# Moving loads, copies and convolution taps between the steps of the first attention in a two-block transformer kernel

## The reference, cut to what matters

```python
h = rmsnorm(x, g_mix)
z = h @ w_in
zb, zc, zx, zq, zk, zv = split(z)              # six pieces of 512 columns
y_c = zb * causal_dwconv3(zc * zx, conv_w, conv_b)
q, k = rmsnorm per head(zq), rmsnorm per head(zk); v = zv      # 8 heads of 64
y_a = dilated_attention(q, k, v)               # 3 branches, merged by their weights
y = concat([rmsnorm(y_c, g_out_conv), rmsnorm(y_a, g_out_attn)])
x = x + y @ w_out
# causal_dwconv3(u, w, b) = u[t-2]*w[0] + u[t-1]*w[1] + u[t]*w[2] + b
```

## Time and profile before

| | us |
|---|---|
| median of 3 runs | 2587.83 |
| the profiled execution | 2583.64 |
| its span | 2582.0 |
| busy in the span: PE, PEld | 2516.0, 2088.5 |
| busy: DVE, ACT, POOL | 1361.7, 1055.3, 1265.2 |

### The profile page before, as it was taken

One profiled execution on the slowest core, in us unless ns is written; L12 is line 12 of the kernel. 1 busy time (PEld: TensorE's weight loads), 2 busy tenths in 40 slices (PEclk: granted clock), 3 DMA queues, 4 the chain that ended last, 5 costly groups with the idle time before them and its releaser, 6 DMA issues.

```text
span 2582.0 us, 34606 instructions
## 1 busy us (share of the span) xinstructions
PE 2516.0 (97%) x12210; PEld 2088.5 (81%) x12210; DVE 1361.7 (53%) x2479; ACT 1055.3 (41%) x1951; POOL 1265.2 (49%) x940
## 2 busy tenths in 40 slices
PE   8989999999999999999999999889999999999999
PEld 6877878888888888888877777689888888888887
DVE  5327766188766762225267888777247333333222
ACT  6336653253333332224256666586234333322120
POOL 2122323457766665534525554454356666656441
PEclk9999999999999999999999999999999999999999
DMA  4253432312222244210323212320412222226311
GB/s 157 75 170 117 116 82 83 146 58 106 90 82 88 77 160 175 82 65 27 107 74 94 66 62 70 108 69 21 155 74 74 82 85 79 82 105 222 114 45 70
DMA packets 107402, 246.28 MB, mean 95 GB/s; under 512 B 18880, under 2 KB 40672, under 8 KB 106976
## 3 DMA queue, kind: packets, MB, share of 16 engines
q1 hardware_dynamic: 107232, 244.08, 27.9%
HBM read 184.27 MB, written 55.05 MB: 93 GB/s over the span
## 4 chain that ended last, share of the span: by engine, by line
PE 87%; DVE 4%; ACT 2%; issue 2%; DMA 2%; POOL 2%; SPq 1%; ACTq 0%; DVEq 0%; POOLq 0%
PE PS L965 10%; PE PS L964 10%; PE PS L963 10%; PE PS L701 8%; PE PS L703 8%; PE PS L702 8%; PE PS L981 6%; PE PS L982 6%; PE PS L983 6%; PE PS L1233 2%; PE PS L1213 1%; PE PS L806 1%; PE PS L933 1%; PE PS L935 1%; PE PS L934 1%
## 5 line engine op out<-in xcount | busy, mean ns | idle before, releaser
L701 PE MATMUL PS<-Hh,Wl 128*128 128x512 f32 x1072 | 434.3, 405 | 12.0 <-DVE Hl L1364 9.4
L703 PE MATMUL PS<-Hh,Wh 128*128 128x512 f32 x1072 | 420.7, 392 | 0.0
L702 PE MATMUL PS<-Hl,Wh 128*128 128x512 f32 x1072 | 420.3, 392 | 0.0
L3220 POOL TENSOR_TENSOR Wl<-Wr,Wh 128x512 fp32r<-128x512 f32 (+1 forms) x158 | 209.4, 1346 | 336.0 <-ACT Wh L2320 335.7
L3323 POOL TENSOR_TENSOR RG<-RW,RG 128x512 fp32r<-128x512 f32 x176 | 246.9, 1408 | 130.2 <-ACT RG L2631 130.0
L1807 DVE TENSOR_TENSOR XA<-PS,XA 128x512 f32<-128x512 f32 x192 | 132.4, 691 | 332.5 <-PE PS L983 332.5
L981 PE MATMUL PS<-Hh,RG 128*128 128x512 f32 x704 | 274.1, 389 | 1.6 <-POOL Hl L3419 1.2
L983 PE MATMUL PS<-Hh,RG 128*128 128x512 f32 x704 | 273.9, 389 | 0.0
L982 PE MATMUL PS<-Hl,RG 128*128 128x512 f32 x704 | 273.9, 389 | 0.0
L3323 POOL TENSOR_TENSOR RG<-SW,RG 128x512 fp32r<-128x512 f32 x120 | 165.3, 1377 | 171.5 <-ACT RG L2631 147.0
L965 PE MATMUL PS<-Hh,RG 128*128 128x512 f32 x640 | 249.0, 389 | 0.0
(11 more groups left out here) (365 smaller groups left out, 5145.6 us busy)
## 6 DMA issues: line engine op xcount, KB each, us to landing
RW<-in_wg SPq DMA_DIRECT2D x44, 512.0 KB, 3.7
RW<-in_wu SPq DMA_DIRECT2D x44, 512.0 KB, 4.6
R<-in_wd SPq DMA_DIRECT2D x88, 256.0 KB, 3.0
hgscr<-GB SPq DMA_DIRECT2D x44, 512.0 KB, 2.6
G<-hgscr SPq DMA_DIRECT2D x40, 512.0 KB, 6.8
Wr<-in_wi SPq DMA_DIRECT2D x27, 512.0 KB, 3.4
Wr<-in_wo SPq DMA_DIRECT2D x16, 512.0 KB, 3.3
spill<-X SPq DMA_DIRECT2D x16, 512.0 KB, 2.6
```

Source lines behind the costliest of these rows:

```text
L701: pe.matmul(ps(b), k.Wl[:, s, wc], xh[:, kx, sl], start=kk == 0, stop=False)
L702: pe.matmul(ps(b), k.Wh[:, s, wc], xl[:, kx, sl], start=False, stop=False)
L703: i = pe.matmul(ps(b), k.Wh[:, s, wc], xh[:, kx, sl], start=False, stop=kk == nk - 1)
L3220: i = pool.tensor_tensor(k.Wl[:, s, c], k.Wr[:, s, c], k.Wh[:, s, c].bitcast(F32), ALU.subtract)
```

## The change

On SyncE the keys of head 1 are loaded before the value tiles are stored. On ScalarE the exponential goes ahead of `next_head`; the next head's keys are copied in two halves, at i = 3 and i = 4; `use` stands behind the first step of a unit; the convolution's first tap is an Identity activation with the tap as scale and the bias as bias; the squares stand behind later steps. On VectorE the first tap is gone and taps 1 and 0 and the two products with b are spread over steps of the b unit and the next c unit. GpSimd's additions and SyncE's store of `YC` follow. For j = 3 the order stays nearly as it was.

```diff
 vector: conv_x
-        if half == 0:
-            return
-        ...waits...
-        dve.tensor_scalar(y, k.ZC[:, 2:T + 2], col("conv_w", 8 + j), col("conv_b", j), ALU.mult, ALU.add).then_inc(
-            *up("conv", "cv", 0, j))
 vector: the loop over units
-                taps = {2: lambda j=j: conv_tap(j, 1), 6: lambda j=j: conv_tap(j, 0)} if (c, half) == ("b", 0) else {}
-                walk(8, 2, taps, tick)
+                later = {}
+                if (c, half) == ("c", 0) and j:
+                    later = {2: lambda j=j, b=b: conv_b(j - 1, 1, b)}
+                if (c, half) == ("b", 0):
+                    if j < 3:
+                        later = {6: lambda j=j: conv_tap(j, 1)}
+                    else:
+                        later = {2: lambda j=j: conv_tap(j, 1), 6: lambda j=j: conv_tap(j, 0)}
+                if (c, half) == ("b", 1) and j < 3:
+                    later = {2: lambda j=j: conv_tap(j, 0), 4: lambda j=j, b=b: conv_b(j, 0, b)}
+                walk(8, 2, later, tick)
 scalar: the head's copies
+    def key_part(h, z):
+        if z == 0:
+            act.wait_ge(*at("k1_in", h, 1))
+        return act.activation(k.KSa[h % 2][:, half_of(z)], k.KSr[:, half_of(z)], ACT.Copy)
 next_head:
+        if i == 3 and h < 7:
+            key_part(h + 1, 0)
         if i == 4 and h < 7:
-            key_high(h + 1)
+            key_part(h + 1, 1).then_inc(*up("q_hi", "k1_hi", h + 1))
 scalar: attention1
-            if s < n:
-                next_head(s)
             if 1 <= s <= n:
                 ...exponential of s-1...
+            if s < n:
+                next_head(s)
 scalar: new
+    def conv_first(j):
+        ...the waits that VectorE had, and zx...
+        act.activation(k.YC[:, j % 2, :], k.ZC[:, 2:T + 2], ACT.Identity, bias=k.col("conv_b", j),
+                       scale=k.col("conv_w", 8 + j)).then_inc(*up("tap0", "cv", 0, j))
+    def conv_square(j, half):
+        staged = [("v2_in", 0, 7), ("v_kept", 7)] if (j, half) == (1, 0) else []
+        square("conv", j, half, k.YC[:, j % 2, half_of(half)], staged + [("yb", j, half)])
 scalar: the loop over units
-            use()
             for half in range(2):
-                walk(8, 2, {}, tick)
+                later = {}
+                if half == 0:
+                    later[2] = use
+                if (c, half) == ("b", 0):
+                    if j < 3:
+                        later[4] = lambda j=j: conv_first(j)
+                    else:
+                        conv_first(j)
+                if (c, half) == ("c", 0) and j:
+                    later[6] = lambda j=j: conv_square(j - 1, 1)
+                walk(8, 2, later, tick)
                 b = bank.next()
+                if (c, half) == ("b", 1) and j < 3:
+                    conv_square(j, 0)
 gpsimd: the loop over units
-                if c == "b" and 0 < j < 3:
-                    add("conv", j, half)
-                    pool.wait_ge(*at("acc", "conv", half, j))
+                if (c, half) == ("b", 1) and 0 < j < 3:
+                    add("conv", j, 0)
+                    pool.wait_ge(*at("acc", "conv", 0, j))
+                if (c, half) == ("c", 0) and 0 < j - 1 < 3:
+                    add("conv", j - 1, 1)
+                    pool.wait_ge(*at("acc", "conv", 1, j - 1))
 sync: tables1
-            if i == 0 and h < 7:
+            if i == 0 and 0 < h < 7:
                 key_load(h + 1)
 sync: before the loop that stores the value tiles
+    key_load(1)
 sync: the store of YC moves from the end of j to the first half of the next j's c unit
+                if (c, half) == ("c", 0) and j:
+                    sp.wait_ge(*at("yb", j - 1, 1))
+                    sp.dma_start(d["yscr"][j - 1], k.YC[:, (j - 1) % 2, :]).then_inc(
+                        *up(("d_ys", j - 1), "yc_stored", j - 1))
```

More of the change, by code:

```diff
@@ L1569, in vector @@
                 if c == "b":
-                    conv_b(j, half, b)
                     if j == 3:
+                        conv_b(j, half, b)
                         add("conv", 3, half, k.sq_no["conv", half, 3])
@@ L2472, in key_high @@
     def key_high(h):
-        act.wait_ge(*at("k1_in", h, 1))
-        act.activation(k.KSa[h % 2][:, :], k.KSr[:, :], ACT.Copy).then_inc(*up("q_hi", "k1_hi", h))
+        key_part(h, 0)
+        key_part(h, 1).then_inc(*up("q_hi", "k1_hi", h))
+    def key_part(h, z):
+        if z == 0:
+            act.wait_ge(*at("k1_in", h, 1))
+        return act.activation(k.KSa[h % 2][:, half_of(z)], k.KSr[:, half_of(z)], ACT.Copy)
     def query_high(h, half):
@@ L2587, in scalar @@
     bg.add(attention1_norm())
+    def conv_first(j):
+        if j == 0:
+            act.wait_ge(*at("zpad"))
+        if j < 2:
+            act.wait_ge(*at("v2_in", 0, 4 + j))
+            act.wait_ge(*at("v_kept", 4 + j))
+        if j >= 2:
+            act.wait_ge(*at("yc_stored", j - 2))
+            act.wait_ge(*at("sq", "conv", 1, j - 2))
+        act.wait_ge(*at("zx", j, 1))
+        act.activation(k.YC[:, j % 2, :], k.ZC[:, 2:T + 2], ACT.Identity, bias=k.col("conv_b", j),
[3 more added lines that the diff above has]
+        square("conv", j, half, k.YC[:, j % 2, half_of(half)], staged + [("yb", j, half)])
     def y_high(half):
@@ L2599, in scalar @@
         for c in "cxb":
-            use()
             for half in range(2):
-                walk(8, 2, {}, tick)
+                later = {}
[9 more added lines that the diff above has]
+                walk(8, 2, later, tick)
                 b = bank.next()
+                if (c, half) == ("b", 1) and j < 3:
+                    conv_square(j, 0)
                 if c == "b":
-                    staged = [("v2_in", 0, 7), ("v_kept", 7)] if (j, half) == (1, 0) else []
-                    square("conv", j, half, k.YC[:, j % 2, half_of(half)], staged + [("yb", j, half)])
                     if j == 3:
+                        conv_square(3, half)
                         y_high(half)
@@ L3698, in sync @@
                     sp.dma_start(k.YR[:, kx, :], d["yscr"][kx]).then_inc(*up(("d_y", kx), "y_in", kx))
-        if j < 3:
-            sp.wait_ge(*at("yb", j, 1))
-            sp.dma_start(d["yscr"][j], k.YC[:, j % 2, :]).then_inc(*up(("d_ys", j), "yc_stored", j))
     def gate_up_load(tag, f):
```

## The result

| | before | changed |
|---|---|---|
| median, us | 2588.56 (4 runs) | 2606.32 (4 runs) |
| lowest to highest | 2584.77 to 2589.59 | 2601.87 to 2609.56 |
| profiled execution, span | 2583.64, 2582.0 | 2605.19, 2603.7 |
| PE busy in the span | 2516.0 | 2526.5 |

The ratio is 1.007, 95% interval 1.0051 to 1.0089: slower by about 18 us. The forecast was 2604, range 2589 to 2615. The row "before" has one run more than the three ahead of the prediction.

The account below looks back on a forecast made before the run. TensorE was taken as busy nearly all the time, so only its waits and slower clock could be won back. 18.0 us won against 33 of query and key stalls and 1 of clock gave +16: 2604 us, range 2589 to 2615.

Parts of the forecast that it names:

- What can be recovered, 19.9 us: TensorE's waits for ScalarE's exponentials and VectorE's PT, 140 to 460 us: 16.9 us, plus 2.0 and 1.0 of slower clock.
- the 18.0 that the forecast counts as won: Attention stage: 19.9 us recoverable, less 0.7 for delayed values and 1.2 for work remaining in the last steps.
- Head 1's keys: Key DMA issued ahead of the value stores: the 7.57 us wait and its clock go, at 0.7 us for delayed values.
- Weights behind a step: ScalarE's use behind each unit's first step shifts GpSimd, fetch and all loads by 3.9 us; queries and keys come late.
- Queries, 7 x 3.0 = 21 us: Heads 1 to 7: late query loads stall TensorE at bank 3 of the outputs, 3.0 us each, range 2.6 to 3.9.
- Keys, 6 x 2.0 = 12 us: Heads 1 to 6: keys due one step earlier stall TensorE's next step 2.0 us more each, range 1.2 to 3.2.
- clock, 1 us: TensorE's slower clock after the new stalls in the attention stage: 1 us, range 0 to 7.
- Sum: Whole kernel: -18.0 + 33 + 1 = +16 us, median 2604, the forecast's own range +8 to +28; chance 0.72.
- That only queries bind: Rival 1: keys come in time and only the query loads cost, -18 + 21 = +3, 2591 us; chance 0.09.
- That the loads have room: Rival 2: query loads land by +9.0, no bank is late and only gains stay, -18, 2570 us; chance 0.13.
- No ACT_TABLE_LOAD stands at the tap: Rival 3 claimed the opposite: Identity needs two table loads around each of four taps, about 2612 us; chance 0.06.

Follow-up runs that it names:

- the kernel with the fetch moved: Changed kernel with SyncE's use(), the weights' fetch that waits for w_lo, moved behind the first attention step's loads: 2565.03 us, ratio 0.991 to the kernel before.
- the kernel whose ScalarE waits for no keys: Changed kernel, use() still late, with both halves of the key copy at i = 4 as before: 2598.96 us, ratio 1.0046 to the kernel before.

## Why the prediction was right, step by step

- **What can be recovered, 19.9 us.** The kernel with the fetch moved has all parts of the change and a span 20.0 us below before (2562.0 against 2582.0). The part to compare with the 18.0 that the forecast counts as won is that from ScalarE's first value tile to the end of the stage: 155.46 to 443.66 before, 154.02 to 424.96 there, 17.2 us less. The other 2.8 lie where nothing was changed.
- **Head 1's keys.** The wait and the slow clock went in the changed kernel. The forecast's price of 0.7 us for the values was low: the trace shows 0.17, 1.20 and 0.52 us of new waits. ScalarE also waited 1.50 us for head 1's first queries, which the forecast had called nothing large; the 0.52 stands behind that. Unit 1's mark is 7.2 us earlier, 6.6 without what lies ahead of the value tiles, against 9.6 - 0.7 = 8.9 foreseen.
- **Weights behind a step.** Weights start 3.2 us after the unit's first transposes (foreseen 3.3), queries are copied 12.4 after (11.7 foreseen for their landing, with 0.3 more in the other units), keys 16.8 after (16.6). The chain is shown from both sides: alone it makes the kernel before 29 to 30 us slower, and undone, on ScalarE or on SyncE, it takes 26 or 41 us off the changed one.
- **Queries, 7 x 3.0 = 21 us.** The waits at L835 for the first output of units 1 to 7 are 3.19, 2.58, 3.21, 3.78, 2.20, 1.96 and 3.35: 20.3. This term is right in place and size.
- **Keys, 6 x 2.0 = 12 us, and clock, 1 us.** These two terms were mis-sized, in opposite directions. For the keys only 1.71, 0.81, 0.71 and 1.01 us of waits for the second output are in the trace, 4.2 in all, and the kernel without their early due time needs 1.4 us less in the seven units and 7 less by the medians; 12 was too much. For the clock, the stretch of 182.5 + 28.9 = 211.4 us is 40.6 more than seven units of 24.4 (the stall-free units 1 and 7 of the kernel with the fetch moved). Recorded waits there are 20.3 + 4.2 + 1.3 = 25.8, so 14.8 lie in no wait, and 12.6 of them in the five units with a low clock. The clock missing in their windows, (0.17 + 0.34 + 0.34 + 0.17 + 0.17) x 10 us, is 11.9. So TensorE at its 1.2 GHz level cost about 12 us where the forecast had 1 and a range of 0 to 7. The slow stretches are not key waits in another form: in unit 4, from the 3.78 us wait to the fourth step's transposes, 6.85 us pass where 4.3 did before, and in the kernel whose ScalarE waits for no keys the same stretch takes 6.57.
- **Sum.** Foreseen +16, measured +17.8 by the medians and +21.7 by the two profiled executions; 2.1 of the latter lie behind the stage. Against the same seven units with the fetch moved (174.5 us) the changed kernel's take 36.9 more, where the forecast's costs were 34. That the total came so near is partly luck: keys and clock together were 4.2 + 12 where 13 stood, with the clock's share far outside its range. The forecast's own range of +8 to +28 had also left out the 7 that it gave the clock as an upper end.
- **Rivals.** That only queries bind (2591) fell as a time with the measured 2606. In kind it came nearer than the forecast gave it: queries and the clock behind them made up nearly all of the cost, and the keys bind clearly only with `use()` at the unit's start (10 us). That the loads have room fell with ScalarE's 32.0 us of waits. No ACT_TABLE_LOAD stands at the tap, an Identity of 1.23 us (foreseen 1.2). By the Trainium skill, "ScalarE: Activation LUTs", section "Table sets: the hidden batching unit", none should; the trace agrees.

## What to carry to other kernels

Before a producer is moved later, read which queue waits for its result and what stands behind that wait: here a 1 us copy moved by 4 us held a DMA queue, and through it the loads of something unrelated. Put the unrelated loads ahead of that wait: this took the changed kernel from 2606 to 2565. The move itself was not needed for the gain. With the loads ahead of the wait, `use()` early or late gave 2566.88 and 2565.03, and without touching SyncE's fetch, `use()` at the start and both key halves at i = 4 gave 2569.92, all against 2587. When a load is needed at step i, moving its consumer to i-1 can cost even if next to nothing waited for it before (here 10 us with `use()` at the unit's start), and it has to be weighed with where the load now is issued.

## What the runs showed of the hardware that was not expected

The length of a wait did not decide whether TensorE's clock fell after it. In the changed kernel no window fell below 1.00 after waits of 3.19 and 2.20 us, while one of 1.96 us, which ended at 353.24, was followed by a granted clock of 0.50 from 354.0 to 357.0; the 1.96 us wait of before was followed by such a stretch too (253.0 to 256.0), and its 2.01 us wait by none. What decides it is not shown. In a kernel with repeated waits of 2 to 4 us this has to be counted as a cost of its own: here about 12 us beside 25.8 us of waits, in five of seven units.

The first tap on VectorE and on ScalarE came out within what can be measured of each other. On VectorE it took 0.81 us each of the four times there, against up to 1.68 in the kernel before, so it was a smaller block than the forecast had priced; why it was shorter was not tested.
